# Middle stage of a two-layer hybrid decoder step: query, value and key projections as three products of high and low parts, and a new order on four engines

## What is computed

```python
z = rmsnorm(x, norm_w) @ w_in          # 1024 -> 3264 columns
q_r, k_r, v_r, g_r, q_lat, c_raw, kpe_raw, g_a = split(z)
o_r, s_new = retention_scan(rope(q_r), rope(k_r), v_r, s0)          # 4 heads of 128
q = (rmsnorm(q_lat) @ w_qb).reshape(.., 4, 128 + 64)                # 384 -> 768
c = rmsnorm(c_raw)                                                  # 256
kn = rmsnorm((c @ w_kb).reshape(.., 4, 128)); v = c @ w_vb          # 256 -> 512 each
o_a = softmax((qn @ kn.T + qp @ kpe.T) * scale, causal) @ v         # prompt
# sample tokens: the same over the cached latents of 16 pages, and the new ones
y = x + concat(silu(g_r) * groupnorm(o_r), silu(g_a) * o_a) @ w_out
```

## Time and profile before

| | us |
|---|---|
| median of 3 runs | 1229.5 (1227.54 to 1229.52) |
| the profiled execution's own time | 1228.56 |
| its span in the trace | 1226.7 |
| PE busy in the span | 1213.5 (99%) |
| DVE, ACT, POOL busy | 728.6, 544.7, 435.0 |
| middle stage, each layer | 111.70 |
| granted clock of PE, whole span | 1.0 (2.4 GHz) |

### The profile page before, as it was taken

How to read it: one execution, slowest core, us unless ns; L and a number is a source line. 1 busy time by engine, 2 the same in 40 slices (tenths; PEclk the granted TensorE clock), 3 DMA queues, 4 the chain that set the end, 5 groups by cost and what they waited for, 6 DMA issues and landing times.

```text
span 1226.7 us, 26265 instructions
## 1 busy us (share of the span) xinstructions
PE 1213.5 (99%) x8727; PEld 1122.3 (91%) x8727; DVE 728.6 (59%) x1379; ACT 544.7 (44%) x1443; POOL 435.0 (35%) x632
## 2 busy tenths in 40 slices
PE   8999999999999999999999999999999999999999
PEld 7999995768999999999999999867789999999998
DVE  5556756565666666676454575656556666665752
ACT  6313235444655555562342132453445555555520
POOL 1033055432554545541001220554235554544500
PEclk9999999999999999999999999999999999999999
DMA  6632104003435422210543130320042543222012
GB/s 219 220 94 61 49 24 115 25 2 95 128 89 156 123 82 75 79 44 30 217 134 112 55 110 1 80 83 1 11 143 78 162 123 97 80 74 83 23 58 67
DMA packets 127687, 107.28 MB, mean 87 GB/s; under 512 B 45713, under 2 KB 123682, under 8 KB 127586
## 3 DMA queue, kind: packets, MB, share of 16 engines
q1 hardware_dynamic: 127586, 106.04, 29.3%
HBM read 95.08 MB, written 10.91 MB: 86 GB/s over the span
## 4 chain that ended last, share of the span: by engine, by line
PE 90%; DVE 3%; SPq 2%; ACT 2%; issue 1%; DVEq 1%; POOL 1%; DMA 0%; POOLq 0%; ACTq 0%
PE ps L1039 28%; PE ps L577 10%; PE ps L578 10%; PE ps L579 10%; PE ps L1014 4%; PE ps L690 3%; PE ps L587 3%; PE ps L588 3%; PE ps L1067 2%; PE ps L1048 2%; PE ps L849 1%; PE ps L703 1%; PE ps L850 1%; PE ps L872 1%; PE ps L1018 1%
## 5 line engine op out<-in xcount | busy, mean ns | idle before, releaser
L2094 DVE TENSOR_REDUCE kss<-ksq 128x8 f32<-128x1024 f32 x128 | 156.0, 1219 | 167.6 <-ACT ksq L1572 167.5
L1572 ACT ACTIVATE ksq<-ps 128x544 f32<-128x544 f32 x256 | 160.2, 626 | 192.8 <-PE ps L1039 192.3
L577 PE MATMUL ps<-w_hi,hT_hi 128*128 128x408 f32 (+2 forms) x704 | 241.8, 343 | 2.1 <-DVE w_lo L1685 2.1
L578 PE MATMUL ps<-w_lo,hT_hi 128*128 128x408 f32 (+2 forms) x704 | 239.2, 340 | 0.0
L579 PE MATMUL ps<-w_hi,hT_lo 128*128 128x408 f32 (+2 forms) x704 | 239.0, 339 | 0.0
L1039 PE MATMUL ps<-wq_hi,cT_hi 128*128 128x272 f32 x1024 | 223.2, 300 | 0.0
L2429 POOL TENSOR_TENSOR krs<-kss_t,cst 128x8 f32<-128x8 f32 x128 | 210.3, 1643 | 20.1 <-issue 4.2
L1039 PE MATMUL ps<-wq_lo,cT_hi 128*128 128x272 f32 x1024 | 211.6, 288 | 0.0
L1039 PE MATMUL ps<-wq_hi,cT_lo 128*128 128x272 f32 x1024 | 211.5, 288 | 0.0
L1039 PEld LDWEIGHTS ps<-wq_hi,cT_lo 128*128 128x128 f32 x1024 | 160.3, 189 | 0.0
L1039 PEld LDWEIGHTS ps<-wq_lo,cT_hi 128*128 128x128 f32 x1024 | 160.1, 188 | 0.0
(11 more groups left out here) (217 smaller groups left out, 2013.4 us busy)
## 6 DMA issues: line engine op xcount, KB each, us to landing
ckv<-in_cache_ckv SPq DMA_DIRECT2D x256, 128.0 KB, 2.0
raw<-in_w_in SPq DMA_DIRECT2D x64, 408.0 KB, 4.7
kp<-in_cache_kpe SPq DMA_DIRECT2D x256, 32.0 KB, 1.8
S<-in_state_ret SPq DMA_DIRECT2D x8, 512.0 KB, 6.5
out<-S SPq DMA_DIRECT2D x8, 512.0 KB, 3.3
wout<-in_w_out SPq DMA_DIRECT2D x8, 344.0 KB, 4.0
z<-in_w_out SPq DMA_DIRECT2D x8, 340.0 KB, 4.6
raw<-in_w_out SPq DMA_DIRECT2D x8, 340.0 KB, 4.4
```

The costliest lines, as they stand in the source:

```text
L577: pe.matmul(out, a_hi, b_hi, start=first, stop=False)
L578: pe.matmul(out, a_hi, b_lo, start=False, stop=False)
L1572: act.activation(ksq[:, q % 2, j, :].rearrange("p (s c) -> p s c", s=2), ps[:, 1 + 2 * j:3 + 2 * j, 0:CUT], ACT.Square).then_inc(kk_sq, 1)
L2094: dve.tensor_reduce(kss[:, hs, 2 * k:2 * k + 2, :], ksq[:, q % 2, :, c0:c0 + HW].rearrange("p j (h k) -> p j h k", h=H), AX.X, ALU.add).th ...
```

## The change

**Projections.** `q_project`, `v_project`, `k_project` and the latent part of `new_scores` become three fp32r products of high and low parts, as the input stage has them. ACT's copy of the turned latents now rounds to fp32r (`ql_hi`, `cl_hi`); DVE gets a new step `latents_lo` that makes the low parts from PSUM; PE waits for `lat_lo` in place of `lat_kept`. The key product uses the split key weights that the page stage already had.

**Weights.** ACT gets `split_projections` (one copy of 1024 columns, three of 768), and DVE four subtractions, between the retention gates and `keep_z(6)`. The low parts overwrite w_vb and w_qb. `decoded_values` needs w_vb again at the layer's end, so SP loads it a second time, behind the first sequence's pages and ahead of the state's store.

**Places.** Buffers are laid out anew; `pr` now shares the place of `gate`, so `probs(0)` waits until all `gates` are done, and `tanh(0)` waits for all latents. `step_scale` runs later.

**Order.** All four lists of calls are replaced.

```diff
+            sp.dma_start(wvb[:, :, :], w_vb.rearrange("l (c p) n -> l p c n", p=P)[L]).then_inc(wvb_again, 16)
             sp.wait_ge(s_ok, S_TILE)
...
             def v_project(t):
-                pe.wait_ge(lat_kept, 3 * (t + 1))
+                pe.wait_ge(lat_lo, t + 1)
...
+                    pe.wait_ge(pw_ok, 1)
                 for c in range(KC):
-                    m = pe.matmul(ps[:, 2, :], cT[:, t % 2, c, :], wvb[:, c, :], start=c == 0, stop=c == KC - 1)
+                    m = product(ps[:, 2, :], (cl_hi[:, t % 2, c, :], cl_lo[:, t % 2, c, :]),
+                                (wvb_hi[:, c, :], wvb_lo[:, c, :]), c == 0, c == KC - 1)
...
                     for c in range(QC):
-                        m = pe.matmul(ps[0:n, half, 0:w], qlT[:, t % 2, c, 0:n],
-                                      wqb[:, c, half * w:(half + 1) * w], start=c == 0, stop=c == QC - 1)
+                        cols = slice(half * w, (half + 1) * w)
+                        m = product(ps[0:n, half, 0:w], (ql_hi[:, t % 2, c, 0:n], ql_lo(t)[:, c, 0:n]),
+                                    (wqb_hi[c][:, cols], wqb_lo[:, c, cols]), c == 0, c == QC - 1)
...
                 for c in range(KC):
-                    m = pe.matmul(ps[0:n, 2, :], cT[:, t % 2, c, 0:n], wkb[:, c, :], start=c == 0, stop=c == KC - 1)
+                    m = product(ps[0:n, 2, :], (cl_hi[:, t % 2, c, 0:n], cl_lo[:, t % 2, c, 0:n]),
+                                (wq_hi[:, c, HQ:HQ + HW], wq_lo[:, c, HQ:HQ + HW]), c == 0, c == KC - 1)
...
+            def split_projections():
+                act.wait_ge(w_lo_ok, N_W * L + 4 * NG)
+                act.activation(wvb_hi[:, :, :], wvb[:, :, :], ACT.Copy).then_inc(pw_hi, 1)
+                act.wait_ge(gr_ok, TILES)
+                for c in range(QC):
+                    act.activation(wqb_hi[c][:, :], wqb[:, c, :], ACT.Copy).then_inc(pw_hi, 1)
...
+            dve.wait_ge(pw_hi, 1)
+            dve.tensor_tensor(wvb_lo[:, :, :], wvb[:, :, :], wvb_hi[:, :, :].bitcast(FP32), ALU.subtract)
+            for c in range(QC):
+                dve.wait_ge(pw_hi, 2 + c)
+                m = dve.tensor_tensor(wqb_lo[:, c, :], wqb[:, c, :], wqb_hi[c][:, :].bitcast(FP32), ALU.subtract)
+            m.then_inc(pw_ok, 1)
             keep_z(6)
...
+            def latents_lo(t):
+                n = rows(t)
+                dve.wait_ge(lat_kept, 3 * t + 1)
+                dve.tensor_tensor(ql_lo(t)[:, :, 0:n], ps[:, 1, 0:QC * P].rearrange("p (c n) -> p c n", c=QC)[:, :, 0:n],
+                                  ql_hi[:, t % 2, :, 0:n].bitcast(FP32), ALU.subtract)
+                dve.wait_ge(lat_kept, 3 * t + 3)
+                dve.tensor_tensor(cl_lo[:, t % 2, :, 0:n], ps[:, 0, 0:KC * P].rearrange("p (c n) -> p c n", c=KC)[:, :, 0:n],
+                                  cl_hi[:, t % 2, :, 0:n].bitcast(FP32), ALU.subtract).then_inc(lat_lo, 1)
...
             latents(0)
             turn_wkb()
+            ret_turn(0)
             q_project(0)
-            ret_turn(0)
```

More of the change, by code:

```diff
@@ L900, in _ @@
             step_read()
+            latents(1)
+            k_turn(0)
+            ret_out(0)
             q_turn(0)
-            latents(1)
-            ret_out(0)
-            k_turn(0)
+            qp_turn(0)
             q_project(1)
-            qp_turn(0)
-            step_update(0)
-            v_project(1)
             scores(0)
             scores(1)
+            step_update(0)
+            turn_probs(0)
+            v_project(1)
+            attend(0)
             step_update(1)
             k_project(1)
-            turn_probs(0)
+            turn_probs(1)
@@ L914, in _ @@
+            latents(2)
+            attend(1)
+            q_turn(1)
             step_update(2)
[L915 to L920, removed]
             scores(2)
             q_project(2)
+            turn_probs(2)
             k_turn(1)
+            scores(3)
+            attend(2)
+            qp_turn(1)
+            step_update(3)
+            scores(4)
+            v_project(2)
             ret_turn(1)
-            scores(3)
@@ L926, in _ @@
-            turn_probs(2)
-            qp_turn(1)
+            turn_probs(3)
+            k_project(2)
+            attend(3)
             ret_scores(1)
[L929 to L935, removed]
             turn_probs(4)
             latents(3)
-            scores(5)
             attend(4)
             q_turn(2)
+            scores(5)
+            ret_out(1)
+            k_turn(2)
@@ L941, in _ @@
+            scores(6)
+            turn_probs(5)
+            qp_turn(2)
             q_project(3)
-            turn_probs(5)
-            scores(6)
-            k_turn(2)
+            v_project(3)
+            attend(5)
+            turn_probs(6)
             ret_turn(2)
-            attend(5)
-            qp_turn(2)
+            scores(7)
+            attend(6)
             ret_scores(2)
[L949 to L953, removed]
@@ L954, in _ @@
             k_project(3)
             turn_probs(7)
+            scores(8)
+            ret_out(2)
+            attend(7)
+            turn_probs(8)
             latents(S_TILE)
[L957 to L962, removed]
+            k_turn(3)
             attend(8)
             q_turn(3)
-            k_turn(3)
+            scores(9)
+            q_project(S_TILE)
+            turn_probs(9)
@@ L966, in _ @@
+            scores(10)
+            qp_turn(3)
+            ret_turn(3)
+            attend(9)
+            k_project(S_TILE)
             ret_scores(3)
-            scores(10)
-            turn_probs(9)
+            scores(11)
+            turn_probs(10)
             ret_out(3)
[L970 to L973, removed]
+            turn_probs(11)
             attend(10)
-            k_project(S_TILE)
-            scores(12)
-            turn_probs(11)
@@ L1439, in probs @@
                 act.wait_ge(sc_max, n + 1)
+                if n == 0:
+                    act.wait_ge(gate_ok, TILES)
                 if n >= 2:
@@ L1983, in clear @@
                 dve.drain()
+            latents_lo(0)
+            gates(0)
             clear()
-            gates(0)
             gates(1)
             gates(2)
-            gates(3)
-            gates(S_TILE)
             sum_q(0)
```

281 lines of the change are left out of this document (160 added, 121 removed).

## The result

The changed kernel takes 1214.9 us in the median of 4 runs (1214.07 to 1215.61), the kernel before 1228.5 (4 runs, 1227.27 to 1229.52): a ratio of 0.9892, 95% interval 0.9881 to 0.9904. The prediction was 1215, in a range of 1208.5 to 1222. The profiled execution took 1214.49 us (span 1212.7), against 1228.56 before: 14.07 less.

A forecast was written before the change was run, and what follows sets the result against it. PE was taken to bound the kernel, busy 99% of the span. From 1228.56 us: -13.8 products + 2 x 0.3 start - 2 x 0.5 order + 0.5 pages = -13.7, 1214.9, predicted 1215; range 1208.5 to 1222.

The forecast's parts named there:

- Products, 13.8: Middle stage: split products for q, v, k and new_scores save 6.9 us of PE a layer, 13.8 in all.
- Order, 0.5 a layer in favour: Middle stage lists: larger waits removed and added about cancel, smaller ones may go; 0.5 us a layer gained, 2 either way.
- the low parts at nothing: Middle stage: four more latents_lo a layer, 5 us of DVE work, hidden if the new lists place them well.
- The second rival: Middle stage: gain given back, PE waiting 10 us if ten tiles each find DVE about 1 us behind; 1225, chance 0.22.
- The end: End of the middle stage: the new order removes PE's waits of 0.41 us before attend(14) and 0.74 before attend(15).
- `k_turn(0)` waits 1.1: Middle stage: PE waits 1.1 us for tile 0's keys, with only step_read and latents(1) ahead of k_turn(0).
- Start of the stage, 0.3: Middle stage's start: q begins 0.9 us late behind tanh and the low part, ret_turn(0) fills 0.6; loss 0.3 a layer.
- Splitting before group 7, nothing: Before input group 7: 3.9 us of DVE weight splitting ahead of keep_z(6) costs nothing, first bank free 3.2 us early.
- Second load of w_vb: SP's feed: first layer's wait for the second sequence's pages grows by 0.5 us, the second layer's stays hidden.
- D: SP's feed: delay from the second w_vb load, issue some 0.5 us plus transfer 1.6, together 2.1 us.
- The rival of the dragging store: SP's feed: state's store completes only after the whole w_vb load of 10.8 us, D 11.3; 1231.8, chance 0.03.

The follow-up runs named there:

- e2: Changed kernel with each projection and new_scores product as one plain fp32 matmul of high parts, low parts made but unused; 1228.6 us, ratio 0.9999.
- The square: Old and new lists, each with plain and split products, low parts always made: e12, e1, e2 and the changed kernel; stages 115.10, 110.34, 111.57, 104.70 us.
- e12: Changed kernel with the earlier kernel's lists, low parts added, and plain fp32 products that leave the low parts unused; 1236.0 us, ratio 1.0060.
- e1: Changed kernel's arithmetic with the earlier kernel's lists on all four engines, five latents_lo put into DVE's list; 1232.7 us, ratio 1.0032 to the kernel before.
- e5b: e1 with latents_lo(3) and latents_lo(S_TILE) each one step sooner in DVE's list; 1228.8 us, ratio 1.0006 to the kernel before.
- e9: Changed kernel with two calls, q_project(3) and q_project(S_TILE), moved sooner in PE's list alone; 1229.8 us, ratio 1.0008 to the kernel before.
- e10: Changed kernel with the end of PE's list as before, attend(14) right behind the first page transposes; 1215.9 us, ratio 0.9899 to the kernel before.
- e8b: Changed kernel with six more DVE steps of 768 columns ahead of keep_z(6); 1223.4 us, ratio 0.9965 to the kernel before.
- e7b: Changed kernel with two more loads, w_qb and w_kb, behind the second w_vb load and ahead of the state's store; 1224.8 us, ratio 0.9973.
- e11: Changed kernel with five more DVE steps ahead of keep_z(6), one fewer than e8b; 1219.4 us, ratio 0.9925 to the kernel before.
- e3: Changed kernel without the third matmul (left low part by right high part) in the projections and new_scores; 1208.3 us, ratio 0.9832 to the kernel before.
- e4: Changed kernel with SP waiting for the state's load to land before issuing the four latents stores; 1215.6 us, ratio 0.9889 to the kernel before.

## Why the prediction was right, step by step

**Products, 13.8: right.** e2 gives 2 x 6.87 = 13.7. Singly, q took 3.27 (3.15 predicted), v 1.48 (1.39), but the plain ones of e2 are longer by as much.

**Order, 0.5 a layer in favour, and the low parts at nothing: right for the new lists, but a small sum of two large terms.** I priced the new lists against the waits of the kernel before, and that difference is near zero (e2: 1228.6, its stage 111.57 for 111.70), within the 2 either way that I gave. The square shows what stands behind this zero: the low parts cost the old lists 3.4 a layer (e12), and the new lists take 3.5 back. "They are hidden if the new lists place them well" carried the gain, and I had given it no price; from the 0.5 I even expected e1 at 1216. It is 17.8 us slower than the changed kernel (11.2 of them in the two stages), e5b 13.9, and e9 shows how narrow the margin is. The second rival (1225) described what happens with lists that are not made for this work. Its 10 us are near the 11.2 of e1's stages, but not by its mechanism: in a layer three of the five tiles wait for low parts, 3.3 us in all, and the rest are other waits.

**The end: right.** The waits 0.41 and 0.74 are back in e10, at 0.6 to 0.9 a layer net of the new 0.34.

**`k_turn(0)` waits 1.1: wrong place.** The keys are ready 0.3 us before PE comes, since PE has waited 1.23 (second layer 0.9) for the state's load. That floor was not in the prediction: in the earlier trace rows `step_read` begins with no wait, at 191.12, just as the load lands. The row of its weight loads in the trace of the kernel before shows it:

```profile
191.12 1.69 PEld L795 LDWEIGHTS ps<-S,qkT 128*32 128x32 f32 x64 [0.76 <-DMA S<-in_state_ret]
```

With slow products the key wait is 0.56 (e2). One wait hid the other.

**Start of the stage, 0.3: right.** q begins at 182.83 (182.75 predicted); from the stage's first transpose, which is 0.17 later than before, that is 2.72 us where 2.81 was predicted.

**Splitting before group 7, nothing: right.** DVE's timeline after has the new steps and `keep_z(6)` behind them, which e8b found to have 3.3 us of slack:

```profile
151.57 1.21 DVE L1835 TENSOR_TENSOR wvb_lo<-wvb,wvb_hi 128x1024 fp32r<-128x1024 f32 x1
152.71 2.68 DVE L1838 TENSOR_TENSOR wqb_lo<-wqb,wqb_hi 128x768 fp32r<-128x768 f32 x3
155.31 2.28 DVE L1748 TENSOR_SCALAR z<-ps,x_root 128x408 f32<-128x408 f32 x4
```

**Second load of w_vb: mis-sized.** D was put at 2.1 us; it is 4.94 - (308.41 - 304.35) = 0.88. The wait of 0.55 did not grow to 1.05 but went. Three terms: D is 1.2 less; PE has 46.0 us of work from `absorb` to that point, where it had 43.7, 2.3 more and not 1.6; and SP went through its page issues in 23.5 us where before it took 25.0, one issue having been held up for 1.8. The rival of the dragging store fell by its size; its mechanism is real (e7b).

The sum came within 0.4 us of the profiled execution's 14.07 partly by luck, because the errors cancel: 1.05 less for the pages, 0.7 more in the stages (0.2), the input stage (0.2) and behind the second stage (0.3).

## What to carry to other kernels

When a change makes one engine's work shorter, ask how far each result's hands stand from their use, not how busy the other engines are: DVE was at 71% here, and two calls moved by a few places cost the whole gain. Price an order together with the work that it is for; here new lists and low parts without the faster products gave 0.0, the faster products in the old lists 4 us of loss, all together 13.6 of gain. A start that shows no wait may still stand exactly on a transfer's landing, so compare it with the landing before counting time saved ahead of it.

## What was not expected of the hardware

PE's granted clock fell from 2.4 to 1.2 GHz behind waits of 1.77 (e1), 1.78 (e11, second layer), 2.18 (e9), 2.83 (e8b), 3.15 (e3), 3.26 (e5b) and 4.13 us (e7b). It did not fall behind 1.79 (e11, first layer), 1.8 (e3, second layer) or, in the first layer of e7b, 2.92. The two waits of e11 stand at the same place of the program and differ by 0.01 us. At the kernel's start PE waits 1.87 us for `w_lo` both in e4 and in the changed kernel, and in the two microseconds from 10 on the clock is 0.56 in e4's profile and 1.00 in the changed kernel's. So the length of a wait does not decide it; what does, these runs don't show. Where it fell, the slower matmuls cost 1.3 to 2.4 us beyond the wait. The Trainium skill ("TensorE: Matmul & The Clock Gate", section The HAM clock gate) has the lower clock as the default that activity lifts. The traces agree in that the clock falls behind idle time and comes back while PE works; the default itself they don't show, since the changed kernel's first microsecond, before PE's first matmul, stands at 1.00.

What stays open: how the 3.6 us a layer that the old lists still lose in e5b divide among the four lists. Swapping one engine's list alone was not run. Nor is it known what the new lists would give without low parts.
